# Zero products at the start, a later load of the angles' constants, and a unit's low products last

## The reference, cut to what matters

```python
mk, mv = jnp.split(mem_n @ w_mem_kv[i], 2, axis=-1)
mixed = jnp.concatenate([mix, mo], -1) @ w_out[i]
x = layer_norm(ALPHA * x + mixed, ln1_g[i], ln1_b[i])
x = layer_norm(ALPHA * x + swiglu(x, w_gate_up[i], w_down[i]), ln2_g[i], ln2_b[i])
```

## Time and profile before

| quantity | us |
|---|---|
| median of 3 runs (lowest to highest) | 1910.05 (1909.97 to 1911.69) |
| span of the profiled execution, first to last instruction | 1906.5 |
| PE busy in it | 1865.8 |
| POOL busy in it | 1516.2 |
| ACT busy in it | 945.2 |
| DVE busy in it | 798.1 |

### The profile page before, as it was taken

The page is one execution under the profiler, slowest core; times in us unless marked ns, Lnnn a source line. Parts: engine busy times, 40 slices in busy tenths (PEclk is TensorE's granted clock), DMA queues, the critical chain, the costliest instruction groups (busy, mean ns, idle before and its releaser), DMA issues.

```text
span 1906.5 us, 27403 instructions
## 1 busy us (share of the span) xinstructions
PE 1865.8 (98%) x9610; PEld 1529.7 (80%) x9610; DVE 798.1 (42%) x1933; ACT 945.2 (50%) x1501; POOL 1516.2 (80%) x1330
## 2 busy tenths in 40 slices
PE   8999999999999999999999999999999999999999
PEld 7878888877888887788887778887887887788877
DVE  6774110456111245411056641106857344455534
ACT  4564444454444445444435544434656654555743
POOL 7768979885897977797987779797686887777785
PEclk9999999999999999999999999999999999999999
DMA  8445656555666554465655456655564564556453
GB/s 292 137 146 178 187 164 223 179 176 145 184 193 214 188 172 149 144 188 164 223 150 157 152 166 187 208 169 174 178 182 122 161 209 152 162 170 178 130 173 111
DMA packets 184558, 330.54 MB, mean 173 GB/s; under 512 B 12221, under 2 KB 44521, under 8 KB 184425
## 3 DMA queue, kind: packets, MB, share of 16 engines
q1 hardware_dynamic: 176512, 323.21, 55.0%
q10 hardware_dynamic: 7912, 5.59, 1.0%
HBM read 325.35 MB, written 3.41 MB: 172 GB/s over the span
## 4 chain that ended last, share of the span: by engine, by line
PE 84%; POOL 6%; DVE 4%; DMA 3%; ACT 2%; issue 1%; SPq 0%; DVEq 0%; ACTq 0%
PE acc L1419 24%; PE acc L1420 23%; PE acc L1426 21%; POOL w_lo L1185 6%; PE tps L1366 4%; PE acc L1441 2%; PE acc L1422 2%; PE ops L1483 2%; PE tps L1459 2%; DMA raw<-in_w_down 1%; PE acc L1390 1%; PE acc L1392 1%; PE acc L1391 1%; DMA raw<-in_w_mem_kv 1%; PE ops L1378 1%
## 5 line engine op out<-in xcount | busy, mean ns | idle before, releaser
L1185 POOL TENSOR_TENSOR w_lo<-raw,w_hi 128x512 fp32r<-128x512 f32 (+2 forms) x1242 | 1475.3, 1225 | 349.9 <-ACT w_hi L1213 348.7
L1213 ACT CAST w_hi<-raw 128x1024 fp32r<-128x1024 f32 (+3 forms) x624 | 615.6, 991 | 745.3 <-PE acc L1426 567.2
L1419 PE MATMUL acc<-w_hi,xT_hi 128*128 128x512 f32 (+1 forms) x1808 | 687.1, 384 | 4.9 <-ACT U L1247 2.9
L1420 PE MATMUL acc<-w_lo,xT_hi 128*128 128x512 f32 (+1 forms) x1808 | 666.6, 372 | 0.0
L1426 PE MATMUL acc<-w_hi,xT_lo 128*128 128x512 f32 (+2 forms) x1744 | 505.2, 371 | 0.0
L1419 PEld LDWEIGHTS acc<-w_hi,xT_hi 128*128 128x128 f32 x1808 | 341.4, 189 | 74.6 <-issue 15.2
L1420 PEld LDWEIGHTS acc<-w_lo,xT_hi 128*128 128x128 f32 x1808 | 342.2, 189 | 52.4
L1426 PEld LDWEIGHTS acc<-w_hi,xT_lo 128*128 128x128 f32 x1744 | 317.8, 189 | 58.2 <-DVE xT_lo L1696 1.1
L1756 DVE TENSOR_TENSOR H<-G,acc 128x512 f32<-128x512 f32 (+1 forms) x48 | 30.9, 643 | 335.5 <-PE acc L1426 335.5
L1419 PE MATMUL acc<-w_hi,hT_hi 128*128 128x512 f32 x352 | 139.5, 396 | 3.6 <-POOL w_lo L1185 3.4
L1420 PE MATMUL acc<-w_lo,hT_hi 128*128 128x512 f32 x352 | 137.2, 390 | 0.0
(11 more groups left out here) (210 smaller groups left out, 1993.5 us busy)
## 6 DMA issues: line engine op xcount, KB each, us to landing
raw<-in_w_gate_up SPq DMA_DIRECT2D x160, 512.0 KB, 3.9
raw<-in_w_in SPq DMA_DIRECT2D x104, 512.0 KB, 3.8
raw<-in_w_down SPq DMA_DIRECT2D x88, 512.0 KB, 3.7
raw<-in_w_out SPq DMA_DIRECT2D x48, 512.0 KB, 3.6
raw<-in_w_in_a SPq DMA_DIRECT2D x32, 512.0 KB, 3.6
raw<-in_w_in_b SPq DMA_DIRECT2D x20, 512.0 KB, 3.7
raw<-in_w_mem_kv SPq DMA_DIRECT2D x16, 512.0 KB, 4.2
raw<-in_w_gate_up SPq DMA_DIRECT2D x32, 256.0 KB, 2.8
```

The source lines that it names most:

```text
L1185: ins = nc.gpsimd.tensor_tensor(w_lo[:, r, i, 0:ch.width], raw[:, r, i, 0:ch.width], w_hi[:, slot, i, 0:ch.width].bitcast(F32), ALU.subtract)
L1213: nc.scalar.copy(w_hi[:, u.u % SPLIT, 0:u.nk, 0:u.chunk.width], raw[:, u.u % RAW, 0:u.nk, 0:u.chunk.width]).then_inc(S["hi_ready"], 1)
L1419: nc.tensor.matmul(o, hi[:, tok], wh, start=first_k, stop=False)
L1420: ins = nc.tensor.matmul(o, hi[:, tok], wl, start=False, stop=False)
```

## The change

Three things change in the code. PE runs 16 products on zeros ahead of its first wait; POOL clears the operand for them, the first tile of `sT_hi`. The three transfers of `ANGLES` are issued by SP and no more by ACT; units 1 and 2 get the priority -1.5 and the angles' constants -1.2, so that they stand between units 2 and 3 in SP's queue, and their estimated cost in the scheduler is 1500 in place of 2500. And in `products`, for token tile 0 of unit 0 and of every unit with no "take" activations (and no turned form), PE waits for the unit's `w_hi` first, computes the terms that don't need `w_lo`, then waits for `w_lo` and computes the hi x weight-lo terms last.

```diff
+WARM = 16
...
-                               ... prio=1 if n >= RAW else -3 if n == 0 else -1, lat=2000)
+                               ... prio=1 if n >= RAW else -3 if n == 0 else -1.5 if n < 3 else -1, lat=2000)
...
-    angles_in = p.task("ACT", "first_constants", None, 2500, "angles_landed", prio=-1, lat=2500,
+    angles_in = p.task("SP", "first_constants", None, 1500, "angles_landed", prio=-1.2, lat=2500,
...
+                elif k.kind == "first_constants":
+                    with nc.allow_non_contiguous_dma(reason="the positions, one to a partition"):
+                        for dst, src in ANGLES:
+                            sp.dma_start(dst, src).then_inc(S["angles_landed"], 16)
...
+            nc.gpsimd.memset(sT_hi[:, 0, :].bitcast(F32), 0.0).then_inc(S["warm_set"], 1)
             for k in order["POOL"]:
...
-                elif k.kind == "first_constants":
-                    with nc.allow_non_contiguous_dma(reason="the positions, one to a partition"):
-                        for dst, src in ANGLES:
-                            act.dma_start(dst, src).then_inc(S["angles_landed"], 16)
...
-                if t == 0:
+                late = t == 0 and not ch.flip and (u.u == 0 or not turned)
+                if late:
+                    pe.wait_ge(S["hi_ready"], u.split.n)
+                elif t == 0:
                     pe.wait_ge(S[u.low.sem], u.low.n)
...
                     nc.tensor.matmul(o, hi[:, tok], wh, start=first_k, stop=False)
-                    ins = nc.tensor.matmul(o, hi[:, tok], wl, start=False, stop=False)
+                    if not late:
+                        ins = nc.tensor.matmul(o, hi[:, tok], wl, start=False, stop=False)
                     if not turned:
-                        ins = nc.tensor.matmul(o, lo[:, tok], wh, start=False, stop=last_k)
+                        ins = nc.tensor.matmul(o, lo[:, tok], wh, start=False, stop=last_k and not late)
                 if turned:
...
+                if late:
+                    pe.wait_ge(S[u.low.sem], u.low.n)
+                    for i in range(u.nk):
+                        ins = nc.tensor.matmul(acc[:, bank, 0:ch.width], act_tile(ch.acts, u.k0 + i)[0][:, P * t:P * t + P],
+                                               w_lo[:, u.u % RAW, i, 0:ch.width], start=False,
                                                stop=u.k0 + i == ch.k_tiles - 1)
...
+            pe.wait_ge(S["warm_set"], 1)
+            for _ in range(WARM):
+                nc.tensor.matmul(acc[:, 3, 0:N], sT_hi[:, 0, 0:P], sT_hi[:, 0, :], start=True, stop=True)
             pe.wait_ge(S["ident_landed"], 16)
```

More of the change, by code:

```diff
@@ L443, in open_chunk @@
             u.load = self.task("SP", "load", u, size * 512 / 300, None,
-                               [self.units[n - RAW].mm[1]] if n >= RAW else [], prio=1 if n >= RAW else -3 if n == 0 else -1, lat=2000)
+                               [self.units[n - RAW].mm[1]] if n >= RAW else [], prio=1 if n >= RAW else -3 if n == 0 else -1.5 if n < 3 else -1, lat=2000)
             u.split = self.task("ACT", "split", u, 195 + 0.835 * size, "hi_ready",
@@ L1026, in build @@
         S = {n: sem(n) for n in (
-            "ident_landed", "angles_landed", "prologue_landed", "rel_landed", "x_landed0", "x_landed1", "mem_landed", "lambda_terms", "lambda_exp", "lambda_done",
+            "warm_set", "ident_landed", "angles_landed", "prologue_landed", "rel_landed", "x_landed0", "x_landed1", "mem_landed", "lambda_terms", "lambda_exp", "lambda_done",
             "angles", "trig_done", "rel_ready", "rel_rows_made", "rel_rows_saved", "bias_landed", "ple_landed", "out_landed", "hi_ready", "lo_ready", "lo_ready_dve",
@@ L1427, in products @@
                                                w_hi[:, u.u % SPLIT, i, 0:ch.width], start=False,
+                                               stop=u.k0 + i == ch.k_tiles - 1 and not late)
+                if late:
[3 more added lines that the diff above has]
+                                               w_lo[:, u.u % RAW, i, 0:ch.width], start=False,
                                                stop=u.k0 + i == ch.k_tiles - 1)
```

## The result

The changed kernel is slower by a little: 1912.33 us (median of 20 runs, 1910.28 to 1915.46) against 1909.3 us (20 runs, 1907.06 to 1911.99) for the kernel before on the same chips. The ratio is 1.0015, with a 95% interval of 1.0009 to 1.0021: about 2.9 us more. I had forecast 0.7 us less. The time lies within the range and nearly all of the interval within 0.2%, but the sign was wrong and the difference is real. Of all runs in this document one, in experiment 6, took 3172.42 us at a granted clock of 0.622; no ratio counts it.

A forecast was written before the change was run, and what follows sets the result against it. Transfers bound the kernel until unit 14 is there, PE from 45.57 us on. Head 0, angles 0, order -0.7 and low last 0 gave span 1905.8, with 3.55 around it 1909.4 us; range 1906.6 to 1912.6.

The forecast's parts named there:

- The head: Kernel start: zero products and earlier loading of x let PE begin unit 1 some 1.2 us earlier, within 0.6 to 1.8.
- Absorbed at unit 14: At unit 14: its transfer's landing stays at 41.74, PE's wait grows from 1.57 to 2.8 us; end gain 0.
- The angles' transfers: DMA and SP's queue: moving the small transfers only moves their loss; 0, bounds -1.2 to +1.1 us.
- Low last: Unit 0 and 48 late units: gain 0, cost 0; other end 3.4 us from the inner wait.
- The order: PE near unit 14: unit 11's second token tile goes ahead and fills the wait; gain 0.7 us, or loss of 1.4.
- Rival 2: SP's queue or PE's order: small transfers cost 1.1 or an unready task 1.4, or both; 1911.2 to 1912.6 us; chance 0.15.
- Rival 3: 48 late units: inner wait stops PE loading the next stationary tile; 0.07 each, 3.4 us, giving 1912.8; chance 0.07.

The follow-up runs named there:

- experiment 6: The kernel before with only the eight constants moved behind unit 15 in SP's queue: 1909.39 us against 1909.25, ratio 0.9999.
- experiment 2: The changed kernel with all three edits, but the angles' task estimated at 0 so the order of before stays: 1909.8 us against 1909.42 before, ratio 1.0002.
- experiment 5: The kernel before with only the angles' transfers moved to SP's queue, other engines in the order of before: 1910.13 us against 1909.25, ratio 1.0005.
- experiment 1: The kernel before with only the changed kernel's order on every engine, angles still issued by ACT: 1912.38 us against 1909.42, ratio 1.0011.
- experiment 4: The kernel before with only the low products last in the 49 units: 1909.67 us against 1909.42, ratio 1.0.
- experiment 9: The changed kernel with the memory rows' first chain moved forward on DVE, PE and ACT: 1910.83 us against 1909.33 before, ratio 1.0007.
- experiment 11: The changed kernel's three edits in the order of before, with the constants behind unit 15: 1906.58 us against 1909.33 before, ratio 0.9986.
- experiment 8: The kernel before with zero products, low products last and constants behind unit 15, angles on ACT: 1908.05 us against 1909.25, ratio 0.9996.
- experiment 7: The changed kernel with ACT's cast of unit 14 moved behind the memory's first two casts: 1911.0 us against 1909.25 before, ratio 1.0014.
- experiment 3: The kernel before with only the 16 zero products added: 1908.8 us against 1909.42, ratio 0.9996.
- experiment 10: The changed kernel in its own order, with the constants behind unit 15 on SP: 1910.41 us against 1909.33 before, ratio 1.0008.

## Why the prediction was wrong, point by point

**The head: right.** I took 1.2 us within 0.6 to 1.8; 0.91 was measured, limited by POOL's `w_lo` of unit 1, as forecast. The zero products ended at 4.88 within the 3.9 to 5.2 given.

**Absorbed at unit 14: right, for the order of before.** Experiment 2 has the landing at 42.44 within 41.2 to 42.5 and a wait of 3.07 where I said 2.8; that the two are so near is partly luck, as only 0.84 of the growth are PE's earlier arrival. I had expected unit 14 to be issued earlier. It was issued later (29.09, in experiment 2 at 29.67, before 28.57), as SP's last issue ahead of it took 1.75 and 2.51 us in place of 0.99; by these durations SP was held back already while issuing. In the changed kernel the gain was absorbed too, but by ACT's wait ahead of unit 12.

**The angles' transfers: right as far as it can be told.** Unit 14's landing stayed. DVE's first use of the positions is at 12.22, within the 11.5 to 12.7 given; ACT's table load at 17.95 and sine at 19.24 are some 0.65 us later than the earlier trace rows, and the first user begins at 20.48 with the sine done, so nothing waits. The 1.2 us that small transfers cost became 1.5, and in experiment 5 unit 14 lands 0.1 later, which is within the scatter of landings.

**Low last: right.** No cost inside (0.24 and 0.23 us), no gain at the down projection: its products still wait 3.3 us for POOL (3.4 in the earlier trace rows).

**The order: here it failed.** I wrote that one product group, unit 11's second token tile, would go ahead of unit 14's and that "at run time this fills 1.37 us of the grown wait", a gain of 0.7, with a loss of 1.4 as the other end. Experiment 1 has for the order alone +2.9 us at the landmark (178.18 against 175.25) and +3.0 between the medians. Two things were wrong in the step. I followed the new estimates for one task on one engine, PE, where they move 153 places on four engines. And I took the product put ahead as free filling, where it was PE's only reserve: the second token tiles of units 10 and 11 went ahead of unit 12, and the memory rows' turning, which feeds units 12 to 15, went 6 us back. Unit 14 itself begins at 46.75, 1.2 us later than the 45.57 that I had kept for it. The bound of 1.4 came from one wait for one task. Here PE waited again at each return of the chains on ACT and DVE: 2.0, 1.4, 0.7, 1.4 and 0.4 us.

Rival 2 had the mechanism nearest to it (an order that isn't ready) at a chance of 0.15 and its price at half; the 1910.05 us that it started from was 0.75 above the 1909.3 of twenty runs, which is why the measured 1912.33 still lies at its upper end. Rival 3 had nearly the time as well (1912.8) with a mechanism that experiment 4 rules out. That 1912.33 lies in the range of 1906.6 to 1912.6 is luck of that start: from 1909.3 the range would have ended at 1911.9.

What stays open: what each single place left in experiment 9 costs by itself, since none was moved alone, what makes up to 2.0 us behind the landmark in some profiled executions, and how often TensorE's clock falls behind the waits at 44 us in either kernel.

## What to carry to other kernels

Where a scheduler writes the order from estimates, an edit of a cost or a priority is an edit of every queue behind it: write both orders out and compare them on all engines before pricing anything, and freeze the order to measure the edit itself (experiment 2 against the change: 2.5 us). A gain ahead of a transfer-bound wait is worth nothing until that wait is moved too: the three edits in the old order gave no measurable change (experiment 2), moving the constants gave none (experiment 6), and all together gave 2.75 us (experiment 11). Without the angles' move the sum stayed within the noise (experiment 8, 1.2 us). Compare a profiled span with its own execution's time, not with the median of others.

## What the runs showed of the hardware that I had not expected

**A wait of 2 us can cost twice.** In experiments 4 and 5 PE waits at unit 14 for 2.03 and 1.98 us, multiplies four products at 0.23 us, and then falls to 0.43 for some 3.4 us. By windows of PE, in experiment 5 (PE, PEclk, DMA share, GB/s):

```profile
44.00:46.00 2.00, 0.33 (x2) 1.00 0.60 166
46.00:48.00 2.00, 2.00 (x8) 0.66 0.01 3
48.00:50.00 2.00, 2.00 (x6) 0.50 0.00 0
```

A granted clock of 0.50 is the lower of TensorE's levels, 1.2 GHz. DVE's first `MKV` behind it is at 61.16, before at 59.46: 1.7 later, of which unit 14's later start is 0.1, so the clock took 1.6. In experiment 4 it is 61.73, with 0.66 by the start and again 1.6 by the clock. After waits of 1.57 (before), 3.07 (experiment 2) and 2.02 us (the changed kernel) the profiled execution kept a granted clock of 1.00 there. So the wait's length doesn't settle it. Whether one kernel has it in some executions only isn't shown, and the spread of the times doesn't tell: the wait is gone in experiments 6, 8 and 11, whose runs lie within 4.5 (without the 3172.42), 2.3 and 3.2 us, and it stands in experiments 4 and 5, within 6.2 and 5.4, but experiment 2, with the longest wait, lies within 3.8, and experiments 7 and 9, with waits of 1.12 and 1.30, within 2.0 and 1.8. Shown are the two executions.

**Zero products did not settle the level at the first products.** Without them, the stretch of slow first products ended at 13.6 us before, in experiment 6 at 13.6, in experiment 4 at 13.1, in experiment 1 at 11.4, and in experiment 5 there was none:

```profile
9.80 0.47 PE L1419 MATMUL acc<-w_hi,xT_hi 128*128 128x512 f32 x1 [0.51 <-DVE w_lo L2041]
10.11 0.39 PE L1420 MATMUL acc<-w_lo,xT_hi 128*128 128x512 f32 x1
```

With zero products the first products were fast after the change and in experiments 2, 8 and 9, and slow until 11 to 12.9 us in experiments 3, 7, 10 and 11, with the same zero products from 1.10 to 4.6 or 4.9 and only turnings between. The Trainium skill ("TensorE: Matmul & The Clock Gate", Part 4: PE-mode transpose) says that transposes do not engage the fast clock; by that rule all eight would be slow at unit 0, and four are. Experiment 5 goes against it too: nothing but sixteen turnings stands ahead of its first product, and that one is fast. Part 1 of the same page of the Trainium skill says that the number of slow products at a start varies from run to run, and that fits all of them. Each kernel has a single profiled execution, so they don't tell how often. Where the level was fast and fell, the column shows it (0.88 from 0.5 to 15 us in those four); where it had not risen yet, as before, it reads 1.00 over products spaced 0.43, and the spacing has to be read.
